# Two output blocks of a second product formed side by side in two PSUM banks, in a two-layer streaming encoder

## What is computed

```python
h = layer_norm(ALPHA * x + y, ln1_g[i], ln1_b[i])          # y: convolution mixer (layer 0), pooling mixer (layer 1)
r = jax.nn.relu(h @ mlp_w1[i])                              # first product: 1024 -> 4096
f = (r * r) @ mlp_w2[i]                                     # second product: 4096 -> 1024
e = (p[i] @ ple_w[i]) * jax.nn.sigmoid(h @ ple_gate_w[i])
x = layer_norm(ALPHA * h + f + e, ln2_g[i], ln2_b[i])
```

## Time and profile before

| | us |
|---|---|
| time, median of 3 runs | 2075.65 (2074.62 to 2076.26) |
| the profiled execution, its own time | 2076.33 |
| its span, first to last instruction | 2074.5 |
| PE (TensorE matmul) busy | 2060.5, 12926 matmuls |
| PEld (weight load) busy | 2057.3, 12926 loads |
| DVE (VectorE) busy | 1457.0 |
| ACT (ScalarE) busy | 963.6 |
| mean granted TensorE clock, share of full speed | 0.997 |

### The profile page before, as it was taken

One profiled execution on the slowest core, in us unless ns is written; L12 is line 12 of the kernel. 1 busy time (PEld: TensorE's weight loads), 2 busy tenths in 40 slices (PEclk: granted clock), 3 DMA queues, 4 the chain that ended last, 5 costly groups with the idle time before them and its releaser, 6 DMA issues.

```text
span 2074.5 us, 32126 instructions
## 1 busy us (share of the span) xinstructions
PE 2060.5 (99%) x12926; PEld 2057.3 (99%) x12926; DVE 1457.0 (70%) x2106; ACT 963.6 (46%) x1493; POOL 24.4 (1%) x39
## 2 busy tenths in 40 slices
PE   9999999999999999999999999999999999999998
PEld 9999999999999999999999999999999999999998
DVE  5332348888777667687788798888776676756576
ACT  4222223555444434446476565645444444355454
POOL 0000000000000000000000000000000000000000
PEclk9999999999999999999999999999999999999999
DMA  4010122443112222234344344421122221343443
GB/s 178 31 61 30 71 92 82 134 145 132 62 60 73 72 82 82 66 117 141 112 142 150 112 160 141 146 93 56 57 82 82 82 82 59 133 161 113 135 142 123
DMA packets 62851, 211.15 MB, mean 102 GB/s; under 512 B 9088, under 2 KB 12288, under 8 KB 62720
## 3 DMA queue, kind: packets, MB, share of 16 engines
q1 hardware_dynamic: 59696, 208.61, 29.5%
q10 hardware_dynamic: 3024, 0.70, 0.2%
HBM read 204.82 MB, written 4.46 MB: 101 GB/s over the span
## 4 chain that ended last, share of the span: by engine, by line
PE 99%; DVE 0%; DMA 0%; ACT 0%; SPq 0%; issue 0%
PE ps L984 33%; PE ps L985 32%; PE ps L986 32%; DMA x_raw<-x_t 0%; PE ps L1044 0%; DVE acc L1611 0%; PE ps L1045 0%; DVE w_split L898 0%; PE ps L1013 0%; PE ps L1050 0%; PE ps L1019 0%; ACT w_split L1215 0%; SPq L923 0%; PE ps L1009 0%; PE ps L1082 0%
## 5 line engine op out<-in xcount | busy, mean ns | idle before, releaser
L984 PE MATMUL ps<-h_hi,w_split 128*128 128x352 f32 x1968 | 635.0, 323 | 0.7 <-DVE acc L1748 0.7
L985 PE MATMUL ps<-h_lo,w_split 128*128 128x352 f32 x1968 | 630.3, 320 | 0.0
L986 PE MATMUL ps<-h_hi,w_split 128*128 128x352 f32 x1968 | 630.0, 320 | 0.0
L984 PE MATMUL ps<-r_hi,w_split 128*128 128x352 f32 x1634 | 527.4, 323 | 4.4 <-DVE w_split L898 4.4
L985 PE MATMUL ps<-r_lo,w_split 128*128 128x352 f32 x1634 | 523.9, 321 | 0.0
L986 PE MATMUL ps<-r_hi,w_split 128*128 128x352 f32 x1634 | 523.6, 320 | 0.0
L898 DVE TENSOR_TENSOR w_split<-w_raw,w_split 128x1024 fp32r<-128x1024 f32 x327 | 390.6, 1220 | 41.7 <-ACT w_split L1215 41.0
L1792 DVE TENSOR_TENSOR acc<-acc,ps 128x352 f32<-128x352 f32 x665 | 327.0, 516 | 125.4 <-PE ps L986 122.8
L1215 ACT CAST w_split<-w_raw 128x1024 fp32r<-128x1024 f32 x327 | 329.9, 1045 | 165.5 <-PE ps L986 162.3
L984 PEld LDWEIGHTS ps<-h_hi,w_split 128*128 128x128 f32 x1968 | 369.0, 187 | 1.6 <-DVE w_split L898 1.0
L985 PEld LDWEIGHTS ps<-h_lo,w_split 128*128 128x128 f32 x1968 | 369.8, 188 | 0.0
(11 more groups left out here) (176 smaller groups left out, 1685.4 us busy)
## 6 DMA issues: line engine op xcount, KB each, us to landing
w_raw<-w_stream SPq DMA_DIRECT2D x375, 512.0 KB, 3.3
x_raw<-x_t SPq DMA_DIRECT2D x4, 704.0 KB, 8.1
y_t<-acc SPq DMA_DIRECT2D x4, 704.0 KB, 6.4
w_raw<-p_t SPq DMA_DIRECT2D x6, 352.0 KB, 3.4
y_t<-acc SPq DMA_DIRECT2D x7, 176.0 KB, 2.0
w_raw<-w_stream SPq DMA_DIRECT2D x3, 256.0 KB, 5.1
x_raw<-x_t SPq DMA_DIRECT2D x4, 176.0 KB, 4.0
x_raw<-x_t SPq DMA_DIRECT2D x2, 352.0 KB, 5.9
```

Of the source, the lines that this page charges most:

```text
L984: pe.matmul(out, wh, mov_h, start=first, stop=False, **more)
L985: pe.matmul(out, wh, mov_l, start=False, stop=False, **more)
L986: return pe.matmul(out, wl, mov_h, start=False, stop=last, **more)
```

## The change

In TensorE's part of a `down` step that has exactly two blocks and isn't `final`, the two blocks are no longer formed one after the other. A new function `side_by_side` goes through the slots, and for each slot issues: high weights of block 0 by high tile, high weights of block 1 by high tile, both blocks by low tile, and both blocks' low weights by high tile. Successive matmuls thus go to the two banks by turns. The wait for the bank of block 1 stands behind the first matmul of block 0. `b_full` is counted by the last matmul of each block, which are now the last two matmuls of the step. The other engines' parts, the plan and the other steps are as before.

```diff
                     pe.wait_ge(r_ready, step.r_need)
-                    for i, m in enumerate(step.blocks):
+                    if len(step.blocks) == 2 and not step.final:
+                        side_by_side(step)
+                    for i, m in enumerate(step.blocks if len(step.blocks) != 2 or step.final else ()):
                         pe.wait_ge(b_free, step.b + (i - 3))
                         for at, end, bank in down_parts(step, i):
                             for f, slot in enumerate(step.slots):
...
+            def side_by_side(step):
+
+                bank, units = B_BANK + step.bank, len(step.slots)
+                outs = [ps[:, bank + i, 0:TG] for i in range(2)]
+                for f, slot in enumerate(step.slots):
+                    r = (step.parts[f // CHUNK], f % CHUNK)
+                    hi, lo = rpart(rh, *r), rpart(rl, *r)
+                    w = [[ws[:, slot, part, m * P:m * P + P] for m in step.blocks] for part in range(2)]
+                    for i in range(2):
+                        if f == 0:
+                            pe.wait_ge(b_free, step.b + (i - 3))
+                        pe.matmul(outs[i], w[0][i], hi, start=f == 0, stop=False)
+                    for i in range(2):
+                        pe.matmul(outs[i], w[0][i], lo, start=False, stop=False)
+                    for i in range(2):
+                        last = pe.matmul(outs[i], w[1][i], hi, start=False, stop=f == units - 1)
+                        if f == units - 1:
+                            last.then_inc(b_full, 1)
```

## The result

The kernel after the change takes 2083.52 us (median of 6 runs, 2081.96 to 2084.34) against 2076.13 for the kernel before (6 runs, 2074.62 to 2077.49). The ratio is 1.0034, with a 95% interval of 1.0023 to 1.0044: slower by 0.34%, 7.4 us, and outside the predicted range. The profiled execution took 2083.55 us with a span of 2081.7, 7.2 us more than the span before.

What follows compares the result with a forecast made beforehand. TensorE's stream of matmuls was taken to bound the kernel, its time being their number by the distance between starts. Median before 2075.65 plus 0 for distance and 1.2 us of new waits gave 2076.9 us, range 2073.5 to 2081.5.

Steps and rivals of the forecast that it cites:

- Part 1: Distance between matmul starts in the 4464 reordered matmuls: taken as unchanged, zero us, between -1.8 and +2.7.
- Part 2: VectorE's adds in changed steps: both come behind the step's end, shifting the work queued behind by 0.28 to 0.5 us.
- Part 3: TensorE waiting for VectorE to free the second bank, mainly near 1215 and 1290 us: 1.2 us, between 0.3 and 2.
- Clock: TensorE's clock level: new waits are shorter than a 0.71 us idle that left it high, so nothing added.
- A: Rival, faster: two banks by turns hide a price of adding to one bank twice; up to 54 us saved, chance 0.07.
- B: Rival, slower: a bank change between every two matmuls costs something; at 2 ns each, 2085.8 us, chance 0.07.
- C: Rival, slower: VectorE falls behind where layers meet, around 1211 to 1226 and 1284 to 1296 us; 2082.3 us, chance 0.07.
- The test I had set: Matmuls between 536 and 915 us: 2388 expected, 2400 or more would be A, 2376 or fewer without listed waits B.

Runs made afterwards that it cites:

- e2: Kernel before with its order of weights and tiles, but matmuls to two banks by turns and the changed kernel's waits and counts: 2077.81 us, ratio 1.0003.
- e7: Kernel before with each triple of the two-block `down` steps reordered to high tile, high tile, low tile: 2076.29 us, ratio 1.0001.
- b3: TensorE alone, network left out; old order, new order and slots by turns, tiles 1536 or 1408 bytes apart at different beginnings: 158.3 to 166.7 ns a matmul.
- b1: TensorE alone, network left out; stretches of 240 matmuls in seven orders, then short cycles: old order 158.9 then 160.0 ns, new 159.8, slots by turns 161.7.
- e3: Kernel before with only the second bank's wait moved behind the first matmul and both counts to the step's end: 2076.85 us, ratio 1.0002.
- e9: Kernel after with every moving tile of the changed steps taken from slot 1's place, 128 bytes past a multiple of 256: 2082.30 us, ratio 1.0029.
- b2: TensorE alone, network left out; old order, new order and first product behind one another, with waits or pauses: old order 160.0 or 158.9 ns, new 159.8.

## Why the prediction was wrong

**Part 1, the distance, failed, and with it the sum.** It was taken as zero, with ends of -1.8 and +2.7 us. It was 5.0: 3.6 in the 4464 matmuls (0.8 ns each) and 1.4 in steps that weren't touched. The step in the argument that failed is the use of the earlier trace rows as the nearest place. I asked only what the change does to banks, and for banks that place was right: e2 shows that they cost nothing. But the change also altered the order of the moving tiles, and in that it is another thing: the first product takes nine matmuls in a row from the tile of one k, where the change takes six from each slot. The order of the operands was never costed as a part of its own, except that the loss of repeated high weights was said to cost nothing, and in that e7 bears it out.

Those rows held a hint that I read wrongly. k = 5 and 7 took 1.42 and 1.43 us, and k = 6, between them, 1.45; I put the difference down to the semaphore waits of k = 6 and kept the cheaper value. But k = 5 and 7 are also the tiles that begin 128 bytes past a multiple of 256, and k = 6 begins on one. 158.3 ns is just what b3 gives for the former, and 161 is the upper of the two levels, 160.0 and 161.1, that b1 and b3 give for the latter. Waits and beginnings go together in these rows, so they can't prove it, but they could have been read as two prices.

The other 1.4 us could not come out of a sum of 4464 times a distance at all: they fell on neighbours. I took the unchanged steps to be unaffected without a word.

**Part 2, VectorE, was right as to the mechanism.** Where it keeps up, the adds now come in pairs behind the step, and the split behind them starts at 572.22:

```profile
571.35 0.95 DVE L1813 TENSOR_TENSOR acc<-acc,ps 128x352 f32<-128x352 f32 x2 [0.97 <-PE ps L1176]
572.22 1.22 DVE L898 TENSOR_TENSOR w_split<-w_raw,w_split 128x1024 fp32r<-128x1024 f32 x1
```

The idle time is one piece of 0.97 us in place of two of 0.43, and the two adds are 0.95 us together, 0.87 us from the first start to the split. The step itself ran about 0.46 us later than before by then, from the distance, so that of the split's 0.75 us (572.22 against 571.47) 0.29 belong to the pair, where 0.28 was said. The idle time ahead of the adds, which I expected to stay near 125 us, is 155.8: that was wrong.

**Part 3, the new waits, was right.** They were foretold for the second bank near 1215.5 and 1290.8 us, 0.37 and 0.31 us. TensorE's timeline of the kernel after, the first three matmuls of each of those steps:

```profile
1219.90 0.77 PE L1172 MATMUL ps<-r_hi,w_split 128*128 128x352 f32 x2
1220.51 0.32 PE L1174 MATMUL ps<-r_lo,w_split 128*128 128x352 f32 x1
...
1295.62 0.71 PE L1172 MATMUL ps<-r_hi,w_split 128*128 128x352 f32 x2
1296.17 0.32 PE L1174 MATMUL ps<-r_lo,w_split 128*128 128x352 f32 x1
```

The first two matmuls take 0.61 and 0.55 us in place of 0.32: 0.29 and 0.23, together 0.5 where 0.7 was said. No others were found, so the total of 1.2 us was 0.7 too high. That they would be listed among TensorE's waits was wrong: they stand only in the timeline. The long waits for split weights stayed at 4.4 us. e3, which has these waits and nothing else, is 1.0002 (0.9993 to 1.0011). The Trainium skill ("Perfetto Trace Analysis", Matmuls) wants independent groups to rotate through the banks; the rotation from step to step was enough for that here.

**Clock.** Right that the new waits don't lower it. Missed was that the fall after the long waits is chance, so that "span of before plus a sum" carries 1.6 us of luck at each of them.

**The rivals.** A: e2 has every bank change of the new order and no gain, so adding to the same bank twice in a row has no price that two banks by turns would save. B ended on the right side, and with the right kind of quantity, a small dearer distance, which was luck, since its mechanism, the bank change, is refuted by e2; and its price of 2 ns per touched matmul was more than twice too high. C did not come: there is no wait near 1211 to 1296 us beyond the 0.5 above.

**The test I had set.** "2376 or fewer with no waits" was to mean B; 2380 was found. A sensible bound would have been worked out from the point from which B decides, 0.66 ns, and from the share of touched matmuls in that window, 54%: 0.22% of 2388, that is 2383 or fewer.

## What to carry to other kernels

When one engine is busy 99% of the time, the distance between its instructions has to be costed first: here half a percent more in a third of the matmuls cost 3.6 us and the new waits 0.5. Each property of the stream that a reorder changes (banks, weights, moving tiles and where these begin in memory) has to be costed by itself, and the place in the trace used as a price has to agree in all of them. Counts of matmuls in fixed windows at an equal granted clock resolve 0.1 ns, and three kernels, each with one of the parts of the change, settle in one go which part it was. Before reordering moving tiles whose pitch isn't a multiple of 256 bytes, look at which beginnings follow each other; and look at the steps that weren't touched too, 1.4 us of the 5.0 were there.

## What the runs showed of the hardware

- The distance of float32r matmuls of 128 x 128 by 352 columns, each with its own weight load, at a granted clock of 1.00: 158.3 ns with all tiles 128 bytes past a multiple of 256 (b3), but 166.7 for a single tile there (b3) and in 28 steps of e9; 160.0 (b3) or 161.1 (b1) with all on a multiple; where they are mixed, 161.7 alternating singly, 159.8 in sixes, and 158.9 or 160.0 in threes.
- The level, where there are two, is kept through short waits (b2), and changed steps put unchanged ones beside them into an upper level: `up` runs went from 158.9 to 160.0 ns in the kernel after and to 160.0 or 161.1 in e9. Why the beginnings matter, and what picks the level, stays open.
- Changing the PSUM bank between every two matmuls has no measurable price (e2: 1.0003, 0.9994 to 1.0012).
- After a wait of 2.2 us TensorE falls to its lower level in some executions and not in others, at 1.6 us each time.
- The Trainium skill ("TensorE: Matmul & The Clock Gate", Back-to-back issue gap) gives N/2.4 + 2.5 ns, 149.2 ns for 352 columns, and calls it the gap of an isolated matmul, which at large N over-counts in a stream of weight loads and matmuls. The traces don't agree for float32r: no order and no beginning tried here came below 158.3.
